# A hybrid scan and MoE layer: one projection stage takes in the modulation, RWKV's inverse grows by predicated copies

## The reference

```python
mod = silu(c) @ w_mod + b_mod              # (6144): shift/scale/gate, twice
modc = silu(c_ctx) @ w_mod + b_mod         # only its first 2048 are used
h = layer_norm(x) * (1 + sc1) + sh1
hc = layer_norm(ctx) * (1 + csc1) + csh1
p, pc = h @ w_in, hc @ w_in                # HGRN2: q i zf zb g, RWKV-7: r k v + low ranks
o_c, s_c = hgrn2_chunk_scan(..context.., 0); o_l, _ = hgrn2_chunk_scan(..latent.., s_c)
y_c, st_c = rwkv7_scan(..context.., 0);      y_l, _ = rwkv7_scan(..latent.., st_c)
# both scans run in both directions; need_ctx is False (DEPTH is 1): o_c and y_c are not used
x = ln_affine(alpha * x + g1 * (concat(readout(o_l, g), readout(y_l, ...)) @ w_out))
x = ln_affine(alpha * x + g2 * hier_moe(h2))   # 64 experts, 2 per token
```

## Time and profile before

| | |
|---|---|
| median of 3 runs | 4801.01 us (4797.78 to 4803.33) |
| profiled execution, its own time | 4793.64 us |
| its span, first to last instruction | 4792.0 us |
| mean granted TensorE clock | 0.938 of full |
| TensorE busy | 4118.3 us (86%) |
| DVE / ACT / POOL busy | 2245.3 / 1140.0 / 1458.4 us |
| 0 to 107 us: before the first TensorE work on tokens | TensorE busy 27.64 |
| 107 to 624: first projection | TensorE busy 474.29 of 517 |
| 624 to 1449: second projection | TensorE busy 770.93 of 825 |
| 1449 to 2877: scans | TensorE busy 1164.13 of 1428 |
| 2877 to 4792: readout, experts, combine | TensorE busy 1681.25 of 1915 |

### The profile page before, as it was taken

One profiled execution on the slowest core, in us unless ns is written; L12 is line 12 of the kernel. 1 busy time (PEld: TensorE's weight loads), 2 busy tenths in 40 slices (PEclk: granted clock), 3 DMA queues, 4 the chain that ended last, 5 costly groups with the idle time before them and its releaser, 6 DMA issues. The chain is left out here.

```text
span 4792.0 us, 108835 instructions
## 1 busy us (share of the span) xinstructions
PE 4118.3 (86%) x40994; PEld 2767.1 (58%) x40994; DVE 2245.3 (47%) x3896; ACT 1140.0 (24%) x2810; POOL 1458.4 (30%) x1647
## 2 busy tenths in 40 slices
PE   2999979999996887888888886786899999998997
PEld 0777856766665777777787773443333333333333
DVE  1111146776764766666666656888111111111115
ACT  0100034444442333333333332321000000000000
POOL 0000001011113656565565643442322222212220
PEclk7999989999998999999999997887899999999998
DMA  9421146555554242423232326431967899999877
GB/s 289 180 71 56 47 126 213 185 196 199 192 184 145 78 132 71 130 74 117 85 117 86 110 62 198 138 131 58 351 254 300 357 381 377 384 395 403 344 276 294
DMA packets 330784, 933.02 MB, mean 195 GB/s; under 512 B 73488, under 2 KB 172176, under 8 KB 281008
## 3 DMA queue, kind: packets, MB, share of 16 engines
q1 hardware_dynamic: 276560, 779.01, 45.4%
q0 software_dynamic: 46944, 131.97, 7.5%
q10 hardware_dynamic: 6912, 16.78, 0.9%
HBM read 970.11 MB, written 209.17 MB: 246 GB/s over the span
## 5 line engine op out<-in xcount | busy, mean ns | idle before, releaser
L2535 PE MATMUL exp_gate_up<-exp_w_gate,exp_rows_and_rowsT 128*64 128x512 f32 x1664 | 743.1, 603 | 49.0 <-DMA exp_w_up<-in_moe_w_up_dram 47.9
L2535 PE MATMUL exp_gate_up<-exp_w_up,exp_rows_and_rowsT 128*64 128x512 f32 x1664 | 743.9, 604 | 0.0
L2535 PEld LDWEIGHTS exp_gate_up<-exp_w_gate,exp_rows_and_rowsT 128*64 128x64 f32 x1664 | 229.3, 139 | 533.9 <-issue 533.8
L738 PE MATMUL rwp_product<-rwp_hT,rwp_w_rw 128*128 128x256 f32 (+1 forms) x2016 | 443.1, 383 | 0.0
L2486 DVE TENSOR_TENSOR exp_hidden<-exp_hidden,exp_gate_up 64x512 f32<-64x512 f32 x104 | 71.9, 692 | 749.7 <-ACT exp_hidden L2467 749.7
L1574 POOL TENSOR_TENSOR rw_A_level<-rw_A_rho_beta,const_level_masks 128x512 f32<-128x512 f32 x216 | 308.9, 1440 | 358.1 <-DVE rw_A_rho_beta L1602 311.4
L738 PEld LDWEIGHTS rwp_product<-rwp_hT,rwp_w_rw 128*128 128x128 f32 (+1 forms) x2016 | 380.3, 189 | 61.0
L891 PE MATMUL hgp_product<-hgp_hT,const_w_hg 128*128 128x256 f32 x1728 | 393.7, 383 | 15.7 <-DMA hgp_hT<-s_hT 15.7
L2560 PE MATMUL exp_down<-exp_w_down,exp_hiddenT 128*64 128x512 f32 x1664 | 380.0, 598 | 1.2
L891 PEld LDWEIGHTS hgp_product<-hgp_hT,const_w_hg 128*128 128x128 f32 x1728 | 326.6, 192 | 70.4 <-DMA hgp_hT<-s_hT 16.1
L2467 ACT ACTIVATE exp_hidden<-exp_gate_up 64x512 f32<-64x512 f32 x104 | 61.3, 589 | 973.6 <-PE exp_gate_up L2535 973.6
(11 more groups left out here) (392 smaller groups left out, 7294.6 us busy)
## 6 DMA issues: line engine op xcount, KB each, us to landing
exp_w_gate<-in_moe_w_gate_dram SPq DMA_DIRECT2D x208, 1024.0 KB
exp_w_up<-in_moe_w_up_dram SPq DMA_DIRECT2D x208, 1024.0 KB
exp_w_down<-in_moe_w_down_dram SPq DMA_DIRECT2D x104, 2048.0 KB
s_rw_in<-prep_operands SPq DMA_DIRECT2D x72, 514.0 KB, 4.1
rw_operands<-s_rw_in SPq DMA_DIRECT2D x72, 514.0 KB, 6.9
hg_qkf<-s_hg_in SPq DMA_DIRECT2D x36, 768.0 KB, 8.5
rw_tokens<-s_rw_tm SPq DMA_DIRECT2D x144, 192.0 KB, 3.9
mod_w<-in_w_mod_dram SPq DMA_DIRECT2D x24, 1024.0 KB, 26.1
```

Of the source, the lines that this page charges most:

```text
L738: mm = nc.tensor.matmul(mp[o % 2][0:width, 0:GROUP], w_in[:, k, c0 - 5 * D_HG:c0 - 5 * D_HG + width], hT[b][:, k, :], start=(k == 0), stop ...
L2535: i = nc.tensor.matmul(pgu[u][q:q + BLK], xT[:, k, r * BLK:(r + 1) * BLK], w[r][:, k, :], start=(k == 0), stop=(k == KD - 1))
```

## The change

1. `modulation` is no stage any more. A class `Modulation` does its work inside `rw_projection`. w_mod is loaded part by part into the memory of `const_w_hg`, before the HGRN2 columns. Part 0 (shift and scale 1) is multiplied ahead of group 0's products, and its two rows are turned into columns by four transposes and added to a bias that is loaded as columns, so that nothing goes through memory. Parts 1 and 2 are multiplied after the products of groups 0 and 1.
2. What the context does not need is left out: 5 of 14 output tiles in group 0 of the first projection, 4 q tiles and 2 g tiles in group 0 of the second, and the loads of these; their places hold zeros.
3. In the scans A is used whole, and R grows by copies under the level's mask: DVE `copy_predicated` of A's blocks at level 0 onto an identity that ACT writes, of the bank's blocks at levels 1 to 5. POOL's level products are gone. The state's decay goes from DVE to POOL. The last chunk's `state` is left out.
4. `RW_ORDER` is as it was; the steps `inverse` and `turned` of level 0 get earlier times.

The core of the diff (its new class is shown by the methods that the steps speak of):

```diff
@@ Modulation, DVE at the start, ACT's and DVE's copies, PE @@
+    def dve_start(self, dve):
...
+        dve.wait_ge(s["sigmoid_done"], 1)
+        nc.vector.tensor_tensor(self.cs[:].rearrange("p k r -> p r k"), self.cols[:], self.sg[:], ALU.mult).then_inc(s["silu_done"], 1)
+        dve.wait_ge(s["lb_loaded"], 64)
...
+    def pe(self, pe, b):
+        if b == 0:
+            pe.wait_ge(s["silu_done"], 1)
+        elif b == 1:
+            pe.wait_ge(s["part_copied"], 4)
+        else:
+            pe.wait_ge(s["rows_added"], 4)
+        for k in range(KD):
+            if k % 2 == 0:
+                pe.wait_ge(self.got[k // 2], 32 * (b + 1))
+            for j in range(4):
+                mm = nc.tensor.matmul(self.acc[32 * j:32 * j + 2, :], self.cs[:, k, :], self.w[:, k, j * 512:(j + 1) * 512],
+                                      start=(k == 0), stop=(k == KD - 1))
+        mm.then_inc(s["part_done"], 1)
@@ rw_projection @@
+        dead = lambda g, o: isinstance(g, int) and g == 0 and (o < 4 or o == NO - 1)
...
+                mod.load_c(sp)
                 load_x(0, 0)
+                mod.load_w(sp, 0)
+                mod.load_rest(sp)
...
                 load_x(2, 0)
+                mod.load_w(sp, 1)
+                mod.pads(sp)
+                mod.load_w(sp, 2)
+                load_x(3, 1)
+                load_x(4, 0)
+                sp.wait_ge(mod.s["part_done"], 3)
...
-                pe.wait_ge(s["cols_ready"], 1)
+                pe.wait_ge(mod.s["ident_ready"], 1)
                 turn(0, 0)
+                mod.pe(pe, 0)
+                mod.pe_turn(pe)
                 turn(1, 1)
                 products(0, 0)
+                mod.pe(pe, 1)
                 turn(2, 0)
                 products(1, 1)
+                mod.pe(pe, 2)
@@ HGRN2 projection @@
+def unused(g, kind):
+    return isinstance(g, int) and g == 0 and kind in "qg"
@@ RwkvScan @@
-            pe.wait_ge(s["level_ready"], 6 * m + l + 1)
...
-                i = nc.tensor.matmul(self.pa[d][q, v, j, :], self.al[d][l % 2][q, v, j, :], self.rT[d][q, v, j, :], start=True, stop=True)
+                i = nc.tensor.matmul(self.pa[d][q, v, j, :], self.ar[u][d][q, v, j, 0, :], self.rT[d][q, v, j, :], start=True, stop=True)
...
+        def ident(d):
+            s = self.s[d]
+            wait(act, s["u_psum"], 2 * m - 2)
+            nc.scalar.activation(self.r[u][d][:].rearrange("p v j t -> p (v j) t"), self.K["idc"][:].unsqueeze(1).broadcast_to([P, 2 * NPAIR, RW_C]),
+                                 ACT.Copy).then_inc(s["ident_ready"], 1)
...
+        def decay(d, v):
+            s, c = self.s[d], 2 * m - 2 + v
+            pool.wait_ge(s["s_order"], c + 1)
+            nc.gpsimd.tensor_tensor(self.st[d][:], self.st[d][:], self.ch[v][d][:, 2 * XW:HEAD].unsqueeze(2).broadcast_to([P, NPAIR, RW_C]),
+                                    ALU.mult).then_inc(s["s_ready"], 1)
...
+                steps += [(rw_time(f"state_{x}", d, 2.6), lambda d=d, v=v: decay(d, v)) for d in range(2)]
...
-                V.tensor_tensor(flat(r[:]), flat(r[:]), flat(self.pa[d][:]), ALU.add).then_inc(s["grown" if l < 5 else "r_ready"], 1)
+                new = heads(self.pa[d][:])
+            dve.sem_inc(self.dve_turns, 1)
+            V.copy_predicated(heads(self.r[u][d][:]), level, new).then_inc(s["grown" if l < 5 else "r_ready"], 1)
...
-        steps += [("gram1a", 2.7, lambda d: inverse(d, 0)), ("gram1b", 2.8, lambda d: turned(d, 0))]
+        steps += [("gram1a", 1.5, lambda d: inverse(d, 0)), ("gram1a", 2.2, lambda d: turned(d, 0))]
```

374 lines of the change are left out of this document (216 added, 158 removed).

## The result

The changed kernel takes 4628.23 us (median of 4 runs, 4613.56 to 4641.90), the kernel before beside it 4799.40: the ratio is 0.9649, 95% interval 0.9612 to 0.9687, so 171 us less. The profiled execution took 4629.26 us, its span is 4627.6 against 4792.0 before, and the mean granted clock is the same (0.939 and 0.938).

The account below looks back on a forecast made before the run. TensorE was taken as busiest everywhere, the start bound by a 24 MB transfer, the scans idle for 215 of 1240 us. Start -44, second projection -18 and scans -50 made -112: 4688 us, range 4640 to 4742.

Parts of the forecast that it names:

- The start: Up to the first projection's end: first product 52 us sooner, group 0 17.4 less, parts 1 and 2 25.6 more: -44.
- the second projection: Group 0 without four q and two g tiles: -18 us, bounds 6 and 27, part given back as waits for VectorE.
- the scans: RWKV and HGRN2 scans, 16 of 18 couples: -30 GpSimd waits, -15 X, -5 masks and R turned: -50 us.
- The "issue" waits stay: Scans: 98.9 us of TensorE's idle time without a named partner, claimed unchanged, so put at nothing.
- The named waits: TensorE's scan waits: 36.3 us GpSimd operands, 27.3 kappas' masks, 23.3 X, 18.9 R turned; 50 counted as gone.
- the scans' 1.8 us per couple: VectorE's scan instructions (L513), freed of GpSimd's level products, come near their minimum: 1.8 us per couple for the two.
- Rival (b): Everything better: scans gain 95 us with VectorE unblocked, bounds' loads cost less; 4644 us, chance 0.13.
- Level 0 early: Level 0 copies ahead of the kappas' masks: 0.7 us late, twice for direction 1; waits there still shrink by 5.
- The bounds for the copy: Predicated copy of 512 columns in the scans: 686 to 880 ns, 700 taken; at most 36 us in all.
- Rival (d): Slower: level 0 copies and additions behind them blocked by GpSimd, 171 us against 112; 4860 us, chance 0.03.
- Rival (a): Scans give nothing back, GpSimd's waits becoming waits for ACT; 4739 us, chance 0.17.
- The 5 us for the single elements: Start: loads of 4096 bias and 2048 bounds elements behind w_mod part 0, estimated at 5 us, bounds' operation at 33.5.

Follow-up runs that it names:

- beside copies: Changed kernel plus twelve unused GpSimd copies of a 128x512 constant per couple, one SBUF operand read: 4638.03 us, ratio 0.9693.
- beside memsets: Changed kernel plus twelve unused GpSimd memsets of 128x1370 per couple, which read nothing: 4647.65 us, ratio 0.9698.
- the kernel with all tiles: Changed kernel whose second projection multiplies all 14 tiles of group 0 again, q and g included: 4636.15 us, ratio 0.9656.
- the kernel with all put back but the copies: Changed kernel plus twelve unused GpSimd products per couple that TensorE waits for, decay on VectorE, level 0 copies behind the kappas' masks: 4683.41 us, ratio 0.9784.
- the old scans: Changed kernel with the scans of the kernel before, new projections kept: 4724.57 us, ratio 0.9860.
- an experiment whose scans had gained nothing: Changed kernel with levels 1 to 5 as one VectorE operation on R and the bank, leaving R at level 0: 4571.65 us, ratio 0.9531.

## Why the prediction was wrong

The sum had -112, the span shows -164. The start and the second projection together gave 52 of the 62 forecast, the scans 102 of 50, and 10 came behind the last HGRN2 scan, where the sum had nothing.

**Scans: -50 forecast, -102 measured; here lies the error.** The step that failed is "The "issue" waits stay, since TensorE's list in a couple is what it was", and with it TensorE's busy time, which the sum left unchanged without giving a reason. The named waits were sized about right: from the first to the last HGRN2 scan those with a releaser fell from 120.9 to 66.9 us, 54 for the 50 forecast, though by other shares (GpSimd 35.0 and X 23.3 gone whole, R turned 23.6 to 3.1, the kappas' masks up from 25.0 to 40.9). The rows "issue", put at nothing, fell from 110.0 to 82.3, and the busy time, put at nothing, from 1085.1 to 1066.0.

What stands behind these terms is shown in part. GpSimd's products cost more than the waits that name GpSimd: put back unused they bring 77 us, and 63 of these vanish when GpSimd does not read, together with 79 us of VectorE's time in the differences, the scan and the copies at level 0. The prediction had named that mechanism, and yet set the scans' 1.8 us per couple only against the level 0 copies and left VectorE's other lines out. So a longer VectorE shows itself on TensorE as waits for masks and for R turned, too. That the rows "issue" of the kernel before were such waits is argued and not shown, and so is the cause of the busy time. Rival (b), "VectorE freed from blocking brings 95 in the scans", was right in the scans and got 0.13. The prediction had named scans under 1330 us and a second projection that does not shorten as what would make it wrong, and both came: the scans' stage took 1323 us (1397 to 2720).

The Trainium skill (SBUF — State Buffer, section Who interferes with whom) states that a VectorE instruction with two SBUF inputs contends with a GpSimd instruction that reads SBUF, and not with one that only writes it. The scan bears out both halves here: it takes 1984 ns beside products, 1370 beside copies, 1212 beside memsets. That the later one is blocked in full, as I had put it, these medians neither show nor exclude: the scan is 771 ns longer beside products of 1276 ns, as it would be if it began when a good third of one was done.

**Level 0 early.** I had the step at -5 over all waits there ("0.7 us late for direction 0, ... less the 1.8 of the scans"). The wait for the kappas' masks rose from 27.3 to 44.3, and moving the copies back gains 20 us. By VectorE's order a copy and a transpose for each direction, four operations of 0.7 us, stand in front of the last two of the kappas' masks, and the transposes I had left out of that count. The copies at level 0 take 0.82 us in the mean, not 0.7.

**Copies and decay.** The bounds for the copy (686 and 880) held: 730, with 700 taken. No price of it is seen beside a free GpSimd. The decay was counted at nothing and is worth some 7 by one profile, little above the spread of profiles. Rival (d), level 0 copies blocked for microseconds, did not come: they take at most 1164 ns. Rival (a), that the scans give nothing back, is refuted.

**Start: -44 forecast, -52.7 measured.** The first product came at 63.9 instead of 69.5: the statistics ran 1.6 us sooner, part 0 took 7.72 instead of 9.69 us, the columns were there 2.6 us after it (42.51 + 7.72 to 52.45 + 0.39) instead of 3, and the products 11.1 behind them instead of 12.5. The time of the lower bounds' first operation (33.5, measured 32.94) was near, and mostly for the reason given: part 0 was put in at 28.5, and SyncE is held at the second load of the bias until 28.09, when it is through. The 5 us for the single elements behind it were an estimate; 4.85 were measured, in which SyncE issues the bounds' loads (2.72) and they land. The kernel with another order of loads shows the other side: with the bounds' loads ahead of w_mod they do not hold VectorE up. Whether single elements in the queue make the hold longer is open: behind bulk loads alone a load of 1 MB went mostly every 2.1 us in the kernel before (once after 6.3), behind a load of single elements none went for 12.7 to 19.9 us. The two gaps with parts 1 and 2 cost 57.4 + 17.4 - 52.7 = 22.1, if group 0's saving is the 17.4 forecast; the forecast was 25.6.

**Second projection, group 0: -18 forecast, -12.8 measured at the next group, nothing at the stage's end.** TensorE waits in the changed kernel at the places where it had products before:

```profile
604.42 2.42 PE L1218 MATMUL prep_bank<-prep_tanh_w,prep_low_rank_w 32*128 32x128 f32 x13 [33.44 <-ACT prep_tanh_w L1146]
613.79 5.46 PE L1000 MATMUL hgp_product<-hgp_hT,const_w_hg 128*128 128x256 f32 x16 [0.73 <-DVEq L981]
678.70 5.44 PE L1000 MATMUL hgp_product<-hgp_hT,const_w_hg 128*128 128x256 f32 x16 [7.96 <-DVEq L981]
```

33.44 instead of 12.21 us for the first tanh, which is itself released by VectorE (L1283), and 7.96 for VectorE in group 1. VectorE was what bound group 0, and it carries its lateness into group 1. The windows from tanh to tanh, of the kernel before and then of the changed one (us, busy us of PE, PEld, DVE, ACT, POOL, granted clock, DMA), show the second part:

```profile
743.39:786.71 43.32, 41.61 (x198) 32.08 (x196) 30.27 (x41) 19.42 (x44) 3.24 (x6) 1.00 0.51 174
786.71:830.27 43.56, 42.45 (x172) 27.77 (x173) 32.69 (x47) 20.27 (x45) 6.51 (x12) 1.00 0.65 215
```

```profile
677.85:724.54 46.69, 44.13 (x200) 34.06 (x200) 31.88 (x46) 19.42 (x43) 5.36 (x10) 0.95 0.60 202
724.54:770.66 46.12, 45.57 (x172) 29.63 (x173) 32.71 (x47) 20.68 (x45) 6.48 (x12) 0.93 0.67 213
```

The third half group is 3.4 us longer, with that wait in it and a granted clock of 0.95 instead of 1.00, the fourth 2.6 us at 0.93. That of the third comes in every profile without the tiles that I read and in none with them, so it belongs to the edit. In the rest of the stage the clock falls to 0.93 for a half group once before and three times more in the changed kernel, and three times in the kernel with all tiles. Whether any of these is the edit's doing, and why, stays open.

**What stays open in the scans:** the 42 us between the kernel with all put back but the copies and the old scans. Their 17 us of idle time may be the shorter way of level 0 or the copies at levels 1 to 5 (that these alone change nothing beside a free GpSimd speaks for level 0, but was not shown beside a busy one), and for their 25 us of busy time, as for the other differences of the granted clock between 0.92 and 0.96, no run shows the cause.

## What to carry to other kernels

A product on GpSimd costs more than the waits that name GpSimd: look for VectorE's lines with two operands in SBUF whose mean lies far above their minimum. Their minimum is no measure of what comes back, though. The differences' median lay 482 ns above their minimum, which for 224 of them is 108 us, and 24 came back. A copy of the work that nobody reads or awaits, with and without its reads, measures the price: here 97 us of VectorE's time and 77 of the kernel's. When work is left out of one engine, ask who was beside it, because its time was hiding someone else's. And when a path gets shorter, place the next step again: the early copies that came with this change cost 20 of the us that it had gained. And where two kernels differ by tens of us, divide the distance into TensorE's busy and idle time first: 20 of the 23 us that looked like an interplay of edits were busy time at another granted clock.

## What the runs showed that I had not expected

- SyncE can be held for 20 us at a load that is not to blame: one load of 2048 single elements is issued in 0.43 us, and the next load, whatever it is, was held for 12.7 to 19.9 us, until what was ahead was nearly through.
- A median within 2% of its minimum (the scan, 1213 ns) is what an instruction looks like that nobody holds up; with products on GpSimd beside it, 1984.
- The time of this kernel depends on its values: 100 expert tiles instead of 104 came with 57 us less for an experiment whose scans had gained nothing.
